# Hybrid decoder trunk on one core: rotation, key compression, norm and start of the attention layers rewritten

## The reference, cut to what matters

```
def rmsnorm(x, g):
    return x * rsqrt(mean(x * x, -1) + 1e-6) * g

def partial_rope(t, cos, sin):                  # first 16 of 64 columns of a head
    t1, t2 = t[..., :8], t[..., 8:16]
    rot = concat([t1 * cos - t2 * sin, t2 * cos + t1 * sin])
    return concat([rot, t[..., 16:]])

def compress(t, pos, w1, w2):                   # 31 blocks of 32 tokens, stride 16
    blk = (t[:, :, tok_idx, :] + pos).reshape(B, G, n_cmp, 32 * 64)
    return gelu(blk @ w1) @ w2                  # w1: 2048 x 256, w2: 256 x 64

def nsa_mixer(h, ...):
    q, kc, vc, ks, vs, kw, vw, gates = split(h @ w_in)
    q, kc, ks, kw = rotated(q) / 8, rotated(kc), rotated(ks), rotated(kw)
    k_cmp, v_cmp = compress(kc, ...), compress(vc, ...)
    # softmax attention over k_cmp, over ks (all blocks are selected at 512 tokens) and over kw
    return (gated sum of the three) @ w_out

for i in range(4):
    x = x + mixer[i % 3](rmsnorm(x))
    x = x + (silu(rmsnorm(x) @ w_gate) * (rmsnorm(x) @ w_up)) @ w_down
return rmsnorm(x)
```

## Time and profile before

| | |
|---|---|
| time, median of 3 runs | 2625.01 us (2621.15 to 2626.06) |
| the profiled execution's own time | 2625.97 us |
| its span, first to last instruction | 2624.2 us |
| TensorE busy | 2512.3 us (96%) |
| VectorE busy | 1440.4 us (55%) |
| ScalarE busy | 903.4 us (34%) |
| GpSimd busy | 299.5 us (11%) |
| chain that ended last: TensorE's share | 87% |
| mean granted TensorE clock | 0.963 of full |

### The profile page before, as it was taken

How to read it: one execution, slowest core, us unless ns; L and a number is a source line. 1 busy time by engine, 2 the same in 40 slices (tenths; PEclk the granted TensorE clock), 3 DMA queues, 4 the chain that set the end, 5 groups by cost and what they waited for, 6 DMA issues and landing times.

```text
span 2624.2 us, 35133 instructions
## 1 busy us (share of the span) xinstructions
PE 2512.3 (96%) x12502; PEld 2110.7 (80%) x12502; DVE 1440.4 (55%) x1969; ACT 903.4 (34%) x1364; POOL 299.5 (11%) x259
## 2 busy tenths in 40 slices
PE   4899999999999999999998999999899999999996
PEld 3777988888888888888877888887777988888885
DVE  6645776644446565343586544447645776644445
ACT  3523554322223333222323322223523554322222
POOL 3200113100003030000023000003200113100003
PEclk8789999999999999999999999999789999999998
DMA  3221001323233233222222323232221001323232
GB/s 110 81 88 49 1 1 41 104 89 104 88 104 113 88 97 103 98 96 97 95 90 90 103 88 104 88 104 96 83 86 49 1 2 41 104 89 104 88 104 96
DMA packets 58713, 213.65 MB, mean 81 GB/s; under 512 B 6512, under 2 KB 6640, under 8 KB 58480
## 3 DMA queue, kind: packets, MB, share of 16 engines
q1 hardware_dynamic: 58464, 211.69, 24.5%
q10 hardware_dynamic: 144, 0.52, 0.1%
HBM read 210.09 MB, written 2.10 MB: 81 GB/s over the span
## 4 chain that ended last, share of the span: by engine, by line
PE 87%; DVE 8%; ACT 3%; issue 2%; DMA 0%; POOL 0%; DVEq 0%; ACTq 0%; SPq 0%; POOLq 0%
PE bank L1265 84%; PE bank L1469 3%; DVE w_lo L752 1%; ACT w_hi L448 1%; DVE xs_lo L760 1%; DVE big L1181 1%; DVE rstat L770 1%; DVE hid_lo L912 0%; ACT big L541 0%; DVE tmp L876 0%; DVE work L879 0%; DVE sm_lo L871 0%; DMA x<-x_in 0%; PE bank L1499 0%; ACT xs_hi L457 0%
## 5 line engine op out<-in xcount | busy, mean ns | idle before, releaser
L1265 PE MATMUL bank<-xs_hi,w_hi 128*128 128x512 f32 x1808 | 714.0, 395 | 16.5 <-DVE xs_lo L760 14.2
L1265 PE MATMUL bank<-xs_lo,w_hi 128*128 128x512 f32 x1808 | 709.9, 393 | 0.0
L1265 PE MATMUL bank<-xs_hi,w_lo 128*128 128x512 f32 x1808 | 709.2, 392 | 0.0
L752 DVE TENSOR_TENSOR w_lo<-raw,w_hi 128x1024 fp32r<-128x1024 f32 x393 | 499.1, 1272 | 235.7 <-ACT w_hi L448 231.2
L448 ACT ACTIVATE w_hi<-raw 128x1024 fp32r<-128x1024 f32 x394 | 413.4, 1049 | 366.4 <-PE bank L1265 239.8
L1265 PEld LDWEIGHTS bank<-xs_hi,w_hi 128*128 128x128 f32 x1808 | 344.0, 190 | 93.1 <-issue 12.3
L1265 PEld LDWEIGHTS bank<-xs_lo,w_hi 128*128 128x128 f32 x1808 | 343.9, 190 | 71.5 <-issue 0.2
L1265 PEld LDWEIGHTS bank<-xs_hi,w_lo 128*128 128x128 f32 x1808 | 343.3, 190 | 72.3
L1265 PE MATMUL bank<-hid_hi,w_hi 128*128 128x512 f32 x720 | 281.9, 392 | 6.1 <-DVE w_lo L752 5.9
L1265 PE MATMUL bank<-hid_lo,w_hi 128*128 128x512 f32 x720 | 281.1, 390 | 0.0
L1265 PE MATMUL bank<-hid_hi,w_lo 128*128 128x512 f32 x720 | 281.1, 390 | 0.0
(11 more groups left out here) (203 smaller groups left out, 3068.1 us busy)
## 6 DMA issues: line engine op xcount, KB each, us to landing
raw<-stream SPq DMA_DIRECT2D x394, 512.0 KB, 3.3
x<-x_in SPq DMA_DIRECT2D x1, 2048.0 KB, 8.3
out<-big SPq DMA_DIRECT2D x8, 256.0 KB, 2.2
big<-consts SPq DMA_DIRECT2D x1, 512.0 KB, 9.9
work<-b_s ACTq DMA_DIRECT2D x1, 512.0 KB, 4.0
tmp<-positions SPq DMA_DIRECT2D x1, 256.0 KB, 10.2
par<-params SPq DMA_DIRECT2D x1, 113.0 KB, 2.1
```

The costliest lines, as they stand in the source:

```text
L752: nc.vector.tensor_tensor(w_lo[:, slot, :], raw[:, k, :], f32(w_hi[:, slot, :]), ALU.subtract).then_inc(w_lo_ready, 1)
L1265: return nc.tensor.matmul(out_, w, v, start=start, stop=stop)
```

## The change

Everything is rewritten between the start of the kernel and the attention of an NSA layer, together with the norm of all nine places.
- Rotation: VectorE multiplies the bank by cos, exchanges rows by its own shuffle instruction (`stream_shuffle`, from PSUM to SBUF), multiplies by a signed sine, and adds. The swap matmuls and both splits are gone.
- Compression: w1 and w2 are used as plain float32. ScalarE copies such a block to `w_f`, VectorE only sets a flag, and `compress` does 4 float32 matmuls of 256 columns for a block. The blocks of w1 alternate with those of the queries (ORDER); the gates come next, then w2. The hidden layer is turned by TensorE.
- Keys: VectorE makes the low parts of block j in a group of four (`key_low`), after ScalarE has made all high parts, and a step later than before.
- Norm: TensorE sums in float32 and for the columns only (`norm`), the roots are taken of 8 columns, VectorE spreads them on diagonal matrices, and a float32 matmul with ones gives the row (`norm_row`), a block later. GpSimd leaves its last addition to TensorE.
- Start: x comes in 8 pieces, ScalarE issues the loads of the first two weight blocks and takes the first squares.
- Attention: BY_DVE is False for all packs, so ScalarE copies all.

```diff
+ORDER = "QWQWQWQWQWWQWQWQ"
-BY_DVE = [r >= 5 for _, r, _ in PACKS]
+BY_DVE = [False for _ in PACKS]
...
-            sp.dma_start(raw[:, 0, :], stream[0]).then_inc(raw_full[0], 16)
-            sp.dma_start(x[:, :, :], x_in).then_inc(x_full, 16)
-            sp.dma_start(raw[:, 1, :], stream[1]).then_inc(raw_full[1], 16)
+            for m in range(MT):
+                sp.dma_start(x[:, m, :], x_in[:, m, :]).then_inc(x_full[m], 16)
...
+                dst = w_f if type(b) is int and b in plan.plain else w_hi
+                nc.scalar.activation(dst[:, slot, :], raw[:, k, :], ACT.Copy).then_inc(w_hi_ready, 1)
...
+                if type(b) is int and b in plan.plain:
+                    nc.vector.memset(flag[:, k:k + 1], 0.0).then_inc(w_lo_ready, 1)
+                    return
...
-                rsqrt_steps(vstat[:, :], rstat[:, :], both, norm_step, 5 * n)
+                rsqrt_steps(vcol, rstd, ncol, norm_step, 5 * n)
+                nc.vector.tensor_tensor(diag, ident[:, :].unsqueeze(1).broadcast_to([P, TT, P]),
+                                        rcol[:, :, 0:1].broadcast_to([P, TT, P]), ALU.mult).then_inc(diag_ready, 1)
...
+                def rotate(b, rho, dst, blocks=1):
+
+                    src = bank[b % RING][:, :]
+                    wait_past(dve, rotated, rho)
+                    dve.wait_ge(block_done, b + 1)
+                    nc.vector.tensor_tensor(tmp[:, 2, :], src, work[:, 0, :], ALU.mult).then_inc(rot_a, 1)
+                    nc.vector.stream_shuffle(work2[:, 1, :], src, SWAP).then_inc(taken, blocks)
+                    dve.wait_ge(taken, b + blocks)
+                    nc.vector.tensor_tensor(work2[:, 1, :], work2[:, 1, :], work[:, 1, :], ALU.mult
                                             ).then_inc(rot_b, 1)
...
                     nc.vector.tensor_tensor(dst, tmp[:, 2, :], work2[:, 1, :], ALU.add).then_inc(rotated, 1)
...
+                for j in range(MIXED, GATE):
+                    split_after(B + j, (B + j) % RING)
+                    if j == MIXED:
+                        finish(MIXED - 1)
+                        key_low(MIXED - 2)
+                    if j == MIXED + 1:
+                        key_low(MIXED - 1)
+                        dve.wait_ge(cm_full, 8 * (a + 1))
+                    if j - 1 in Q_AT:
+                        q = Q_AT.index(j - 1)
+                        rotate(B + j - 1, 14 * a + 6 + q, tile(qf, q), Q_AT[q + 1] - Q_AT[q])
...
                 for t in range(TT):
-                    mm(bank[5][:, 2 * t:2 * t + 2], sq_hi[:, bass.ts(t, P)], ones[:, 0:2], True, False)
-                    last = mm(bank[5][:, 2 * t:2 * t + 2], sq_lo[:, bass.ts(t, P)], ones[:, 0:2], False, True)
+                    mm(bank[5][:, 2 * t:2 * t + 2], work[:, 0, bass.ts(t, P)], f32(ones[:, 0:2]), True, False)
+                    last = mm(bank[5][:, 2 * t:2 * t + 2], last_sq[:, bass.ts(t, P)], f32(ones[:, 0:2]), False, True)
                 last.then_inc(norm_sum, 1)
+
+            def norm_row(n):
+
+                pe.wait_ge(diag_ready, n + 1)
+                mm(bank[4][:, :], f32(ones[:, :]), diag.rearrange("p t q -> p (t q)"), True, True
+                   ).then_inc(row_sum, 1)
...
+                    for k in range(4):
+                        kt = 4 * (c % 4) + k
+                        last = mm(bank[6 + v][:, 0:2 * P], cm[:, v, bass.ts(kt, P)],
+                                  w_f[:, b % RING, bass.ts(k, 2 * P)], kt == 0, kt == 15)
```

More of the change, by code:

```diff
@@ L66 @@
 ROPE_STEPS = 13
+SQUARES = 2 * MT - 2
 PAR = {}
@@ L668, in sgu @@
                         b = B + 4 * half + j
+                        if half == 0 and j == 3:
+                            row(n)
                         if half == 0 and j == 2:
@@ L710, in pool @@
                 out_projection(l)
-            split(0)
+            for b in range(RAW):
+                act.dma_start(raw[:, b, :], stream[b]).then_inc(raw_full[b], 16)
             act.wait_ge(par_full, 16)
@@ L741, in _ @@
                 ffn(l)
-            sum_split(plan.norms - 1)
             root(plan.norms - 1)
+            row(plan.norms - 1)
         @block.vector
@@ new lines, in key_low @@
+                def key_low(j):
+                    dve.wait_ge(key_hi_ready, 4 * (4 * a + j - KS + 1))
+                    for half in range(2):
+                        at = ((j - KS) // 2, 2 * (j % 2) + half, slice(None))
+                        rows = slice(64 * half, 64 * half + 64)
+                        for h in range(2):
+                            nc.vector.tensor_tensor(key_lo[(slice(64 * h, 64 * h + 64), *at)], tmp[rows, j % 2, :],
+                                                    f32(key_hi[(rows, *at)]), ALU.subtract).then_inc(key_lo_ready, 1)
@@ new lines, in turn_hidden @@
+                def turn_hidden(v):
+                    pe.wait_ge(ch_full, 2 * a + v + 1)
+                    for k in range(2):
+                        last = nc.tensor.transpose(bank[6 + v][:, bass.ts(2 + k, P)], ch_t[:, v, bass.ts(k, P)],
+                                                   ident[:, :])
+                    last.then_inc(ch_turned, 1)
+                for j in range(MIXED, GATE):
+                    if j in Q_AT:
+                        project(B + j, (B + j) % RING, MT, xs)
+                    else:
+                        compress(W1_AT.index(j))
+                    if j == W1_AT[3] + 3:
+                        turn_hidden(0)
@@ L1684, in _params @@
     put("invf", np.where(d < ROPE_DIM, inv[d % half], 0.0).astype(np.float32)[:, None])
+    put("sign", np.where(d < half, -1.0, np.where(d < ROPE_DIM, 1.0, 0.0)).astype(np.float32)[:, None])
     put("anyvalid", (np.arange(P) >= 31).astype(np.float32)[:, None])
@@ L1696, in _consts @@
     con[:, CON["ident"]:CON["ident"] + P] = np.eye(P)
-    half = ROPE_DIM // 2
-    for h in (0, DH):
-        for f in range(half):
-            con[h + f + half, CON["swap"] + h + f] = -1.0
-            con[h + f, CON["swap"] + h + f + half] = 1.0
     con[:, CON["causal"]:CON["causal"] + P] = np.where(r[None, :] > r[:, None], NEG, 0.0)
```

427 lines of the change are left out of this document (168 added, 259 removed).

## The result

| | before | after |
|---|---|---|
| time, median (4 runs each) | 2624.16 us (2621.15 to 2626.06) | 2524.15 us (2523.44 to 2524.56) |
| profiled execution: own time, span | 2625.97, 2624.2 us | 2523.96, 2522.2 us |

The ratio is 0.9622 with a 95% interval of 0.9608 to 0.9635: 100 us faster. The forecast was 2516 (2494 to 2540), 8 us too fast.

What follows compares the result with a forecast made beforehand. TensorE, busy 96% of the span, was taken as the bound. Gains up to the attentions, 62.1 and 47.9 us after waits, less 5.3 for other norms, plus 0.5 and 4.2, made 109.4 us: 2516 us, range 2494 to 2540.

Steps and rivals of the forecast that it cites:

- The bound and the places: Up to the attention in both NSA layers: TensorE waits for VectorE before blocks 10 and 12, 4.6 and 8.1 us.
- the ring: Key steps: ScalarE's copies and split, VectorE's split and rotation form a cycle of 7.7 us, against TensorE's 5.43.
- GpSimd in the ring: Key steps 3 to 6: position additions beside VectorE add 1.7 us a layer, bounds 0 and 4.3; full blocking 6.5.
- The low clock behind a wait: After each TensorE wait before blocks 10 and 12: slower matmuls cost about 1.7 us.
- The start: Kernel start: x's first eighth at about 4 us, low parts end 17.5; first attention at 155.3 without waits, 78.3 earlier.
- The wait before the row: First norm: TensorE finishes blocks 0 and 1 by 25.4 us, row's matmul at 33.1, block 2 counted from 36.5.
- The attention: Attention of both layers: moving all copies to ScalarE, 44 a layer at 0.60 us, costs nothing.
- Other norms and the end: Four FFNs and SGU lose 5.3 us; the pooling layer gains 0.5 and the end 4.2.
- The w1 matmuls: Compression: a w1 block is 8 float32 records of 0.215 us, 1.72 us; eight blocks take 13.8.
- The shuffle: VectorE's rotation: one shuffle takes 0.68 us, lower bound 0.43, upper 2.3.
- the rival of a longer ring: Key steps: shuffle at 2.3 us, five rotations a layer, or GpSimd blocking in full; 8 to 25 us more, 18%.
- The rival without waits: Key steps: copies overlap better or the shuffle costs 0.43 us, so no waits; 34 us less, 2482, 17%.

Runs made afterwards that it cites:

- Experiment 1: Changed kernel, but in the key steps ScalarE rounds the next weight block before copying the rotated tile: 2490.33 us, 33.8 less.
- experiment 2: Changed kernel with the low parts of block 7 computed behind the first query's rotation, not ahead of it: 2518.13 us, 6.0 less.
- experiment 3: Changed kernel with GpSimd's eight position additions cut to 4 elements a partition, first NSA layer only: 2521.35 us, 2.8 less.
- experiment 9: Changed kernel with GpSimd adding the squares of x only after VectorE's eight low parts of x: 2524.75 us, no gain.
- Experiment 6: Changed kernel with the first two weight blocks queued behind pieces of x, and ScalarE's table loaded early: 2520.87 us, 3.3 less.
- Experiment 7: Changed kernel with the angle chain and both sines moved behind the first norm's diagonals and row: 2523.66 us, 0.5 less.
- Experiment 4: Changed kernel with the attention's copies shared between VectorE and ScalarE again, as before: 2525.27 us, no difference.
- Experiment 5: Changed kernel with every rotation's shuffle run twice, the second over the first: 2534.28 us, 10.1 more.
- experiment 8: Changed kernel with the edits of Experiment 1 and experiment 2 together: 2486.39 us, 3.9 less than Experiment 1 alone.
- experiment 10: experiment 8 plus x ahead of the weights and the squares' additions behind the low parts of x: 2484.86 us, 1.5 less than experiment 8.
- experiment 11: experiment 8 plus x ahead of the weights and the angle chain behind the first norm: 2485.38 us, 1.0 less than experiment 8.

## Why the prediction came out as it did

**The bound and the places: right.** The waits stand before blocks 10 and 12 in both layers, ended by the shuffle, in a ring of copies, weight split and rotation. The ring's steps were forecast at 7.7 us, and 6.5 with a flag; without GpSimd beside them they took 7.73 and 6.71. Waits of 4.6 and 8.1 us plus 1.7 for GpSimd were forecast, 14.4 together; 7.11 and 8.07 were measured in the second layer, 15.2. (The forecast's own terms give 2.72 us for a rotation where it writes 2.77, and 7.6 for the step where it writes 7.7; nothing hangs on it.) Experiment 1 shows that the ring makes the waits, experiment 2 that the low parts make 2.8 us of each second one.

**GpSimd in the ring: under-sized.** I took 1.7 us a layer; experiment 3 has 2.4 in the ring and 2.8 to 3.1 in all. The Trainium skill (SBUF — State Buffer, SBUF: two separate sides) has the two engines wait for each other's whole instructions. The angle steps of experiment 9 look like that: a VectorE step and an addition took turns, one pair in 1.40 us. In the ring of the changed kernel the price was smaller than the 6.5 us a layer that I derived from the rule. All four VectorE operations that I had counted did run beside additions (1.33 us where undisturbed), but only the two of the rotation paid much, 1.03 and 0.93 us; the two weight splits paid about 0.15 each, and the product and the shuffle that read PSUM nothing. At the splits it was GpSimd that waited: the split ran from 67.67 to 69.04 us, and the addition that began at 67.92 took 2.31 us. So the one that comes second pays, about 1 us here, and I had put every wait on VectorE.

**The low clock behind a wait: under-sized.** I took 1.7 us. From its first matmul to the next block's, block 10 took 7.90 and block 12 7.77 us in the first layer, 7.38 and 7.23 in the second, each for 5.43. That is 8.6 us over the four waits for my 6.8, 1.8 more.

**The start: the step that failed.** "Its first eighth should be there at about 4 us": it landed at 7.22, beside 1 MB of weights on ScalarE's queue, and a table load of 1.28 followed, which I had not counted. VectorE's low parts of x began at 11.36, not 7.2, and took 11.6 us where I had put 10.3, so they ended at 22.97 for 17.5. From there on the forecast holds: two splits 2.3 us for 2.5, the angle chain 7.0 for 7.2, and the row's matmul came at 37.86 for 33.1, 4.8 late. The forecast for the first layer has block 0 rotated at 36.5 + 5.0, less the 1.6 us that it gives VectorE there, so at 39.9; it came at 44.87, 5.0 late. That is two thirds of the 7.3 us. From there to the read of block 8's bank the ring took 59.2 us for a forecast of 58.1 (61.4 less 5.0, and 1.7 for GpSimd), 1.1 more, over half of it GpSimd's; and from block 12 to the attention it is 74.6 for 73.5, another 1.0, 0.6 of it the low clock of block 12.

Experiment 6 confirms that the weights beside x delay its pieces (4.38 for 7.22), and it takes the table load out of the way. Yet it gives back only 1.5 us at the low parts and the row, because VectorE's program has the low part of the first weight block ahead of those of x, and that block lands at 7.6 now. What is left, 2.7 us until the low parts begin (9.85 for 7.2) and 1.3 in their length, was not taken apart further; experiment 9 shows that without GpSimd's sums beside them they take 0.75 us each instead of 1.45 on average.

**The wait before the row: right, with little effect.** The low clock fell where it was forecast, on the row (2.07 us for 1.02 elsewhere) and the start of block 2. Experiment 7 finds no cost of either beyond half a us while the ring is there.

**The attention: right.** From the first matmul of the attention to the same matmul of the output projection (373.42, before 428.07) it is 194.7 us for 194.5 in the first layer, and 194.4 for 194.8 in the second. Experiment 4 finds no price either.

**Other norms and the end: right to 1.6 us.** -3.1 for -3.7, and 4.2 for 3.2.

**The w1 matmuls: over-sized.** A w1 block takes 1.54 us from start to start (119.13 to 120.67), not 1.72: 1.4 us a layer too much, which hid a part of the misses above; that the total came within 8 us owes something to this and to the other norms and the end.

```profile
119.13 1.89 PE L1225 MATMUL bank<-w_f,cm 128*128 128x256 f32 x8
120.67 0.58 PE L1225 MATMUL bank<-xs_hi,w_hi 128*128 128x512 f32 x1
```

**The shuffle: right.** 0.68 forecast, 0.732 measured. The estimate of 0.6 from the Trainium skill (VectorE: DVE Perf Modes, The perf-mode tier table) is a fifth under that. Experiment 5 prices the rival of a longer ring: seven shuffles a layer count, not the five that I wrote, and had the shuffle taken 2.3 us, 1.6 x 14 = 22 us more would have come.

**The rival without waits** (2482) was wrong as a forecast, but it is nearly what experiments 8, 10 and 11 reach, 2484.9 to 2486.4, mainly by another order of the same instructions.

## What to carry to other kernels

When two engines hand a tile back and forth while both also prepare the next weights, write the cycle down from one rotation to the next, not each engine's load: here VectorE was busy for 45.5 and ScalarE for 32.1 of the 70 us from 40 to 110, and moving one 1 us instruction ahead of four others in each key step gave 30 to 34 us. Before removing a wait, ask what sets the pace behind it: taking away the 6.6 us ahead of the row gave half a us with the ring (experiment 7) and one without it (experiment 11, with x ahead besides). Work moved out of one contention needs a look at what it is moved beside: here additions moved away from instructions of 0.75 us, which had grown by 1.0, came to lie beside ones of 0.43, which grew by 0.9.

## What the runs showed of the hardware that was not expected

VectorE's one-source operation in SBUF of 512 columns took 1.37 us beside GpSimd's float32 additions and 0.43 alone (experiment 9); the three-operand low part of x about 1.77 and 0.75; a product and a sum of two SBUF tiles 1.71 and 1.62 for 0.69, a shuffle from PSUM 0.73 both ways. Of eight DMAs of 256 KB issued one after another from one queue, each issue took 0.58 us, and the first was used at 7.22 us while a second queue moved 1 MB, at 4.38 once that was put behind it. Float32 matmuls of 256 columns between blocks of fp32r matmuls ran in a stage at clock 0.92, and at 0.98 once the waits were gone, where a run of 128-column fp32r ones had been at 0.50. Behind waits of 6.7 to 8.1 us the next 24 matmuls took 1.8 to 2.5 us more than the 5.43 of an undisturbed block, and behind waits of 2.0 and 2.3 us (experiment 1) still 1.7 to 1.8 more.
